# Last SSD layer of a hybrid backbone: where and when its first two output weight units are split

## The reference

```
z, xbc, dt = split(h @ w_in)                      # w_in: 1024 x 6208
xs, B, C   = split(silu(depthwise_conv5(xbc)))    # xs: 2048 wide, 32 heads in 8 groups
y          = chunked scan over 128-token chunks, forwards and backwards, + xs * d_skip
out        = rms_norm(y * silu(z)) @ w_out        # w_out: 2048 x 1024
x          = layer_norm(alpha * x + gate * out)
```

## Time and profile before

| | |
|---|---|
| median of 3 runs | 1557.35 us (1554.51 to 1560.70) |
| the profiled execution's own time | 1556.7 us |
| its span, first to last instruction | 1555.5 us |
| outside the span | 1.2 us |
| TensorE matmul busy | 1464.3 us, 94% |
| VectorE busy | 1129.3 us, 73% |
| ScalarE busy | 711.1 us, 46% |
| GpSimd busy | 326.1 us, 21% |
| mean granted TensorE clock | 0.975 of 2.4 GHz |

### The profile page before, as it was taken

How to read it: one execution, slowest core, us unless ns; L and a number is a source line. 1 busy time by engine, 2 the same in 40 slices (tenths; PEclk the granted TensorE clock), 3 DMA queues, 4 the chain that set the end, 5 groups by cost and what they waited for, 6 DMA issues and landing times.

```text
span 1555.5 us, 22694 instructions
## 1 busy us (share of the span) xinstructions
PE 1464.3 (94%) x8557; PEld 1211.7 (78%) x8557; DVE 1129.3 (73%) x1680; ACT 711.1 (46%) x1271; POOL 326.1 (21%) x379
## 2 busy tenths in 40 slices
PE   5889999999998999999899999999998999999987
PEld 3778888888877888876568887877787888888865
DVE  0688999999976376767638545635536999999996
ACT  1554554455534353555544423222424556555562
POOL 1043344443441011001000000000000244434440
PEclk7899999999989999999999999999999999999999
DMA  9245544556442312315332335444241343443443
GB/s 322 74 139 163 166 120 147 163 163 176 124 142 99 122 57 76 117 42 163 108 109 95 116 129 190 126 145 157 80 136 41 104 120 109 130 115 109 121 134 125
DMA packets 169420, 197.38 MB, mean 127 GB/s; under 512 B 9696, under 2 KB 151648, under 8 KB 169312
## 3 DMA queue, kind: packets, MB, share of 16 engines
q1 hardware_dynamic: 158480, 163.08, 33.6%
q0 software_dynamic: 9296, 30.19, 7.4%
q10 hardware_dynamic: 1536, 2.67, 0.5%
HBM read 194.59 MB, written 1.31 MB: 126 GB/s over the span
## 4 chain that ended last, share of the span: by engine, by line
PE 46%; DVE 35%; issue 8%; ACT 7%; DMA 2%; POOL 1%; SPq 0%; DVEq 0%; ACTq 0%; POOLq 0%
PE ps L415 12%; PE ps L417 12%; PE ps L416 12%; DVE xc L903 7%; DVE w_lo L384 5%; DVE cum_b L911 4%; PE ps L444 2%; ACT Wb L766 2%; ACT w_hi L377 2%; DVE Wb L930 2%; DVE Hs L948 1%; PE ps L596 1%; PE ps L469 1%; PE ps L602 1%; PE ps L1890 1%
## 5 line engine op out<-in xcount | busy, mean ns | idle before, releaser
L415 PE MATMUL ps<-h_hi,w_hi 128*128 128x512 f32 (+2 forms) x1088 | 412.0, 379 | 8.9 <-DVE w_lo L384 5.6
L417 PE MATMUL ps<-h_hi,w_lo 128*128 128x512 f32 (+2 forms) x1088 | 399.2, 367 | 0.0
L416 PE MATMUL ps<-h_lo,w_hi 128*128 128x512 f32 (+2 forms) x1088 | 398.8, 367 | 0.0
L384 DVE TENSOR_TENSOR w_lo<-raw,w_hi 128x1024 fp32r<-128x1024 f32 (+1 forms) x205 | 247.4, 1239 | 123.9 <-ACT w_hi L377 122.2
L377 ACT ACTIVATE w_hi<-raw 128x1024 fp32r<-128x1024 f32 (+1 forms) x205 | 208.9, 1050 | 144.9 <-PE ps L417 119.0
L415 PEld LDWEIGHTS ps<-h_hi,w_hi 128*128 128x128 f32 (+1 forms) x1088 | 205.8, 189 | 54.9 <-issue 20.5
L417 PEld LDWEIGHTS ps<-h_hi,w_lo 128*128 128x128 f32 (+1 forms) x1088 | 205.5, 189 | 34.0
L416 PEld LDWEIGHTS ps<-h_lo,w_hi 128*128 128x128 f32 (+1 forms) x1088 | 206.1, 189 | 31.1
L903 DVE SCALAR_TENSOR_TENSOR xc<-ps,gp,xc 128x508 f32<-128x508 f32 (+1 forms) x224 | 162.7, 727 | 18.0 <-ACT xc L735 12.0
L417 PE MATMUL ps<-w_hi,ylo 128*128 128x512 f32 x384 | 150.8, 393 | 0.0
L415 PE MATMUL ps<-w_hi,h_hi 128*128 128x512 f32 (+1 forms) x336 | 120.7, 359 | 4.4 <-issue 2.8
(11 more groups left out here) (258 smaller groups left out, 2607.9 us busy)
## 6 DMA issues: line engine op xcount, KB each, us to landing
raw<-in_mod_w SPq DMA_DIRECT2D x80, 512.0 KB, 4.7
raw<-in_ssm_w_in SPq DMA_DIRECT2D x64, 512.0 KB, 4.9
cum_b<-cum_scratch POOLq DMA_DIRECT2D x96, 256.0 KB, 5.7
raw<-in_ssm_w_in SPq DMA_DIRECT2D x66, 256.0 KB, 4.4
raw<-in_ssm_w_out SPq DMA_DIRECT2D x32, 512.0 KB, 4.8
raw<-in_pool_w_in SPq DMA_DIRECT2D x32, 512.0 KB, 4.7
raw<-in_attn_w_in SPq DMA_DIRECT2D x20, 512.0 KB, 3.9
raw<-in_pool_w_out SPq DMA_DIRECT2D x16, 512.0 KB, 4.6
```

The costliest lines, as they stand in the source:

```text
L384: dve.tensor_tensor(lo[:, 0:width], raw[:, r % RS, 0:width], hi[:, 0:width].bitcast(F32), ALU.subtract).then_inc(lo_done, 1)
L415: pe.matmul(o, hi_s, hi_m, start=first, stop=False)
L416: pe.matmul(o, hi_s, lo_m, start=False, stop=False)
L417: return pe.matmul(o, lo_s, hi_m, start=False, stop=last)
```

## The change

1. The list of loads: in the last layer, out 0 stands right behind x(6) and out 1 right behind x(7), and not behind z(7).
2. The place: the two units leave the ring of four. Unit u takes the context half of rows 8u to 8u+7 of `ylo` (four rows for the high part, four for the low), so it is written and read in runs of 256 elements, 512 apart. ScalarE waits for the third `x_p` count of the layer, since these rows had held its early units. All later units take the ring slot of the unit that came two later before.
3. The time of the split: ScalarE and VectorE split out 0 as the last work of the sixth step (i = 5) and out 1 as the last of the seventh (i = 6). The old places (ScalarE at the end of the eighth step, VectorE in the drain) are gone.
4. `LAST_CHUNKS` (always 4), `halves` (always both) and `parts` (always the whole row) are new arguments whose values give the instructions of before.

```
@@ the order of the units
             for i in range(GRP):
                 add_piece("w", L, "x", i)
+                if last_layer(L) and i >= GRP - 2:
+                    add("w", L, "out", i - (GRP - 2), 0)
                 add_piece("w", L, "bc", i)
...
-                add("w", L, "out", 2 * a, 0)
-                add("w", L, "out", 2 * a + 1, 0)
+                for c in (2 * a, 2 * a + 1):
+                    if (L, "out", c, 0) not in [key for key, _ in w_units]:
+                        add("w", L, "out", c, 0)
...
-    ring = [key for key, _ in w_units if key not in IS_EARLY]
+    IS_LATE = {(depth - 1, "out", u, 0): u for u in range(2)}
+    ring = [key for key, _ in w_units if key not in IS_EARLY and key not in IS_LATE]
@@ w_place, w_place_free
+        if key in IS_LATE:
+            c = 8 * IS_LATE[key]
+            return [ylo[:, c + 4 * a:c + 4 * a + 4, 0:SEG] for a in range(2)]
...
+        elif key in IS_LATE:
+            eng.wait_ge(lay[key[0]]["x_p"], 3)
@@ ssd_act_step, end of a step
         z_silu(g, 1)
-        if i + 1 == GRP:
+        if last_layer(L):
+
+            if GRP - 3 <= i < GRP - 1:
+                act_split(act, L, "out", i - (GRP - 3), 0)
+        elif i + 1 == GRP:
             for c in (0, 1):
                 act_split(act, L, "out", c, 0)
@@ ssd_dve_step, the drain
             for c in (0, 1):
                 dve_ylo(dve, L, c)
-            for c in (0, 1):
-                dve_split(dve, L, "out", c, 0)
             weigh_steps(0)
@@ ssd_dve_step, end of a step
         if mods:
             dve_mod_col(dve, *mods[1], 6, 256)
+        if last_layer(L) and GRP - 3 <= i < GRP - 1:
+            dve_split(dve, L, "out", i - (GRP - 3), 0)
@@ out_chunk: the same matmuls, with a moving operand and a PSUM row seen as 2 x 256
+            o = bank[2 * n + half]
+            if (L, "out", c, 0) in IS_LATE:
+                w = slice(2 * half, 2 * half + 2)
+                o = o.rearrange("p (a n) -> p a n", n=SEG)
```

More of the change, by code:

```diff
@@ L172, in backbone, with LAST_CHUNKS @@
              3: [("dt", 0, 0), ("x", 0, 0), ("x", 0, 1)]}
+    def LAST_CHUNKS(L):
+        return 4
     items, w_units, m_units = [], [], []
@@ L338, in used @@
         if what == "out":
-            return (s["out_p"], i + 1) if i + 1 < chunks(L) else (s["acc_p"], len(out_tiles(L)))
+            if i >= chunks(L) - LAST_CHUNKS(L):
+                return (s["out_p"], i + 1) if i + 1 < chunks(L) else (s["acc_p"], len(out_tiles(L)))
+            return s["out_p"], i + 1
         if L % 3 == 0:
@@ L359, in w_place, with w_shaped @@
             return [ylo[:, c + 2 * a:c + 2 * a + 2, :].rearrange("p c n -> p (c n)") for a in range(2)]
+        if key in IS_LATE:
+            c = 8 * IS_LATE[key]
+            return [ylo[:, c + 4 * a:c + 4 * a + 4, 0:SEG] for a in range(2)]
         n = RING_OF[key] % WS
         return [w_hi[:, n, :], w_lo[:, n, :]]
+    def w_shaped(key, ap, width):
+        return ap.rearrange("p (a n) -> p a n", n=SEG) if key in IS_LATE else ap[:, 0:width]
     def w_place_free(eng, key):
@@ L376, in act_split @@
         w_place_free(act, key)
-        act.activation(w_place(key)[0][:, 0:width], raw[:, r % RS, 0:width], ACT.Copy).then_inc(hi_done, 1)
+        hi = w_place(key)[0] if key in IS_LATE else w_place(key)[0][:, 0:width]
+        act.activation(hi, w_shaped(key, raw[:, r % RS, :], width), ACT.Copy).then_inc(hi_done, 1)
     def dve_split(dve, *key, width=UNIT):
@@ L383, in dve_split @@
         dve.wait_ge(hi_done, W_OF[key] + 1)
-        dve.tensor_tensor(lo[:, 0:width], raw[:, r % RS, 0:width], hi[:, 0:width].bitcast(F32),
+        if key not in IS_LATE:
+            hi, lo = hi[:, 0:width], lo[:, 0:width]
+        dve.tensor_tensor(lo, w_shaped(key, raw[:, r % RS, :], width), hi.bitcast(F32),
                           ALU.subtract).then_inc(lo_done, 1)
@@ L1420, in first_tiles, with out_chunk @@
         return [3, 0, 1, 2] if L % 3 == 1 else list(range(len(out_tiles(L))))
-    def out_chunk(pe, L, n, c):
+    def out_chunk(pe, L, n, c, halves=(0, 1)):
         s = lay[L]
@@ L1430, in out_chunk @@
         q = slice(128 * tiles[n], 128 * tiles[n] + 128)
-        for half in range(2):
+        for half in halves:
             w = slice(512 * half, 512 * half + 512)
-            last = three_pass(pe, bank[2 * n + half], yhi_of(L, c)[:, q], ylo[:, c, q], hi[:, w], lo[:, w],
-                              c == 0, c == nk - 1)
+            o = bank[2 * n + half]
+            if (L, "out", c, 0) in IS_LATE:
+                w = slice(2 * half, 2 * half + 2)
+                o = o.rearrange("p (a n) -> p a n", n=SEG)
+            last = three_pass(pe, o, yhi_of(L, c)[:, q], ylo[:, c, q], hi[:, w], lo[:, w], c == 0, c == nk - 1)
         if c == nk - 1:
             last.then_inc(s["acc_p"], 1)
-        elif n == order[-1]:
+        elif n == order[-1] and 1 in halves:
             last.then_inc(s["out_p"], 1)
@@ L1466, in pe_out @@
         N, nk = len(out_tiles(L)), chunks(L)
-        for c in range(c0, nk - 4):
+        stretch = nk - LAST_CHUNKS(L)
+        for c in range(c0, stretch):
             for n in range(N):
@@ L1470, in pe_out @@
         for n in range(N):
-            for c in range(nk - 4, nk):
-                out_chunk(pe, L, n, c)
+            for halves in ((0, 1),):
+                for c in range(stretch, nk):
+                    out_chunk(pe, L, n, c, halves)
             if n and L + 1 < depth:
@@ L1676, in dve_norm, with add_and_measure @@
             dve.wait_ge(in_loaded, 64)
-        def add_and_measure(n):
+        def add_and_measure(n, parts=(slice(0, D),)):
             tt = tiles[n]
             u0 = s["base"]["u_d"] + 5 * n
-            dve.wait_ge(s["acc_p"], n + 1)
             r = small[:, 8 + tt:9 + tt] if L % 3 == 0 else 1.0
[L1683 to L1690, removed]
+            for a, c in enumerate(parts):
+                dve.wait_ge(s["acc_p"], n + 1 + a)
+                dve.scalar_tensor_tensor(pair[n][:, c], pair[n][:, c], r, gate_b[:, tt // 2, c],
+                                         ALU.mult, ALU.mult).then_inc(s["u_d"], 1)
+                dve.wait_ge(s["u_d"], u0 + 2 * a + 1)
+                dve.scalar_tensor_tensor(resid[:, tt, c], resid[:, tt, c], ALPHA, pair[n][:, c],
+                                         ALU.mult, ALU.add).then_inc(s["u_d"], 1)
+                dve.wait_ge(s["u_d"], u0 + 2 * a + 2)
+                for h in range(c.start, c.stop, 512):
+                    last = dve.bn_stats(stats[:, tt, h // 512, :], resid[:, tt, h:h + 512])
+            u0 += 2 * len(parts) - 2
             last.then_inc(s["u_d"], 1)
```

## The result

The changed kernel takes 1561.55 us in the median of 20 runs (1558.46 to 1564.84), the kernel before 1557.37 us in 20 runs beside them (1554.51 to 1561.63). The ratio is 1.0021, 95% interval 1.0014 to 1.0028: slower by 2.2 to 4.4 us. The profiled execution took 1559.88 us with a span of 1558.6, 3.1 us more than before's.

What follows compares the result with a forecast made beforehand. VectorE's list was taken to bound the steps. Profiled 1556.7 us, + 6.0 for two steps, - 2.55 in the drain, gave 1560.1; with the median 0.65 above the profiled run, 1560.8 us, range 1555.5 to 1564.5.

Steps and rivals of the forecast that it cites:

- VectorE leads the steps: Last layer's steps: VectorE's list is the bound, with 0.4 us a step of waiting; TensorE trails about a microsecond behind.
- the rival: Sixth and seventh steps: new idle time on TensorE lowers its clock, costing 1.5 us each, 1563.8 us in all; chance 0.17.
- absorbed: Rival for the steps: TensorE is the real bound, so the two steps cost nothing, 1553.3 us; chance 0.05.
- no wait: Rival for the steps: VectorE doesn't lose the 1.86 us, steps cost 2 x 1.13 us, 1557.1 us in all; chance 0.10.
- +6.0 us for the two steps: Sixth and seventh steps: each 3.0 us longer, 1.13 of VectorE work and 1.86 of waiting for ScalarE's high part.
- SyncE's queue: nothing: Load queue: bc's second half lands 4.5 us later in the median, at no cost; up to 1 us for the range.
- The place: nothing: Units stored in four runs of 256: no cost taken; at the other end, the drain's matmuls take 5.9 us more.
- -2.55 us in the drain: Drain without the pair of low parts: 3.1 us gained less 0.55 for `weigh_steps` under GpSimd's products; bounds -3.1 and -2.4.
- a gain under 2 us: Drain: named sign of a wrong prediction, because another wait, GpSimd's products or the exponentials, comes last.
- the chain there is the broadcast DMA, so nothing: End of the eighth step: the 2 us freed on ScalarE bring nothing, since the broadcast DMA is the chain.
- TensorE's clock in the drain: Rival: with less idle time in the drain the clock stays at 2.4 GHz, 1.5 us come back, 1559.3 us; chance 0.30.
- GpSimd's gap of about 5 us: Drain: 4.98 us without releaser ahead of the last broadcast DMA's issue, assumed to stay with GpSimd's list; 1 us either way.

Runs made afterwards that it cites:

- e2: Changed kernel with the moved units' high parts ahead of silu(2) on ScalarE, VectorE's list unchanged; ratio to the kernel before 0.9997.
- e9: Changed kernel with the moved units' low parts only 8 columns wide on VectorE, high parts whole; ratio to the kernel before 1.0004.
- e3: Changed kernel with load list and both splits put back as before, only the units' new place and the ring kept; ratio to the kernel before 1.0003.
- e1: Changed kernel without any edit, profiled a second time; ratio to the kernel before 1.0013.
- e6: Changed kernel with the moved units between bc and z in loads and both lists, in the second and third steps; ratio to the kernel before 0.9984.
- e10: Same code as e6, run once more beside the kernel before; ratio to the kernel before 0.9988.
- e4: Kernel before with the splits of output units 0 and 1 only 8 columns wide on ScalarE and VectorE; ratio to the kernel before 0.9977.
- e7: Changed kernel with GpSimd waiting in the drain for VectorE's first decay before its products that weigh x; ratio to the kernel before 1.0025.

## Why the prediction was right, point by point

Predicted were 1560.8 us, range 1555.5 to 1564.5, and a change within 0.5%; measured 1561.55 and +0.21%. The sign and the size were those of the forecast, and its working can be checked term by term. The closeness of the sum is in part luck. In the profile 1560.1 was forecast and 1559.88 came: the drain gave 0.7 us less than forecast, the time ahead of the layer took 0.3 more, and the clock, which the sum had left alone, gave 1.4 back.

**VectorE leads the steps.** Shown: +3.0 us on VectorE's list is +3.0 us of step, in both steps, and TensorE's waits for VectorE are unchanged. TensorE took its share as new idle time at its transposes (5.1 us in four pieces, put down to "issue"), as the rival said, yet its clock stayed at 1.00 from 1366 to 1486. So neither "absorbed" nor "no wait" came true.

**+6.0 us for the two steps.** Measured +6.03. The split into 1.13 of work and 1.86 of wait is shown from both sides: without the wait a step costs 1.1 (e2, its first), without the work 1.97 (e9, its first, where a narrow instruction of 0.17 us is left). The wait could be read off the rows of before, since `silu(3)` can't begin before VectorE's last tap ends.

**SyncE's queue: nothing.** Right for the change, where bc was late for ScalarE (2.3 us twice) under the cover of VectorE's own delay. It is a cost that waits for that cover to go: in e2, 0.92 us.

**The place: nothing.** e3 shows none within 0.1 us, together with the ring.

**-2.55 us in the drain.** The term that was mis-sized: -1.87 (and -1.76 in e1), outside its bounds of -3.1 and -2.4. From the last broadcast's landing to the scan pass 13.7 us and not 12.2, and a gain under 2 us was a sign of being wrong that the prediction itself had named. Relative to y(7), the first decay starts at 2.71 us in both kernels, the second at 5.92 before and 7.21 now, `weigh_steps` at 14.69 and 11.98, the scan at 20.67 and 18.80. The step that failed is "the chain there is the broadcast DMA, so nothing" for the freed ScalarE. GpSimd got its transposed x earlier, started its products 2.0 us behind y(7) and not 3.3, ahead of VectorE's decay, and held it; the DMA had landed 2.1 us before the second decay ran. That cost 1.0 us at the masks. The two low parts of the rows, no longer beside these products, gave 0.6 of it back (10.40 to 11.99 behind y(7), against 9.41 to 11.59). So `weigh_steps` starts 2.7 us earlier and not 3.1. It came under GpSimd's product as foreseen, but took 2.12 us rather than 1.83. These 0.4 and 0.3 us are the whole of the miss. In e2, without the long decay, the drain is 3.2 us shorter, beyond my bound of 3.1; there the last broadcast also landed early enough (5.03 us behind y(7), 5.90 before) that the second decay didn't wait for it.

**TensorE's clock in the drain** was a rival with 0.30. Its price is what both profiles of the changed kernel show, no fall behind the scan and -1.4 us; its condition, a clock that stays at 2.4 GHz, is not. The fall came earlier, from 1487 to 1491 among the z projections, and there it cost nothing that can be seen: behind them TensorE still sits idle 0.63 us for VectorE's gate (before L612 at 1494.84). The time isn't 1559.3, as the drain gave less and the median of 20 runs stands 1.7 us above the profiled run.

**GpSimd's gap of about 5 us** ahead of its last broadcast is there at the same instruction in all 13 profiles (4.05 to 5.05 us), which fits the assumption that it belongs to GpSimd's list; its cause is open.

## What to carry to other kernels

Where one engine's list is the bound, moving work of two engines costs what the leader waits for the other plus the work. Look where the helper's half would really start in its own list: here a split of 1.1 us cost 3.0, and the same split put where the leader already waited cost 0.0 to 0.8. A unit inserted in a shared load queue also delays its successors; look for the one that another wait is hiding.

## What the runs showed of the hardware

A VectorE instruction with two SBUF inputs can be held for the whole of a chain of GpSimd products. In the changed kernel GpSimd's six 128x256 products took 3.45 us and VectorE's decay, begun 0.7 us behind them, 3.85. It ended 1.1 us behind the last of them, about its own length, so by this estimate it ran only then. In other profiles both give way in part: the six take 5.3 to 6.4 us, the first decay 1.2 to 1.5 and the second up to 1.7. GpSimd and VectorE in the drain of e2:

```profile
1485.83 6.33 POOL L1156 TENSOR_TENSOR xw<-xT,sg 128x256 f32<-128x256 f32 x6 [0.16 <-ACT xT L782]
```

```profile
1486.64 1.45 DVE L938 TENSOR_TENSOR cum_b<-cum_b,sg 128x1024 f32<-128x1024 f32 x1
```

Here GpSimd began 0.8 us ahead, and neither was held for long. Which of the two happens was seen to differ for the same code (e6: 1.45, e10: 4.08 us), with starts only 0.3 us different against each other. The distance of the starts doesn't decide it by itself: with GpSimd 0.2 us ahead the decay took 1.53 us (e9), with GpSimd 0.04 us behind it took 4.02 (e4). What decides it stays open. In the steps from y(1) on the order of the starts does go with it: the second low part of bc took 1.22 us in the four steps where it began ahead of GpSimd's first product (two of e2, one each of e7 and e9), 1.64 in all others of the 13 profiles. The Trainium skill ("GPSIMD Engine Reference", Specifications) says that the two engines contend for the SBUF interfaces when VectorE has two SBUF inputs; the trace agrees, and shows that the contention can be all on VectorE's side.
